# Dealing the index score matmuls of block 2 among the products of the forget-gate load

## What is computed

```
h = rmsnorm_2(x, norm_mix[layer])
hq, hf, hi, hg, sq, sk, sv, iq, ik, iw, mq = split_in(h @ w_in[layer])
...
# sparse attention: which 128 keys a query keeps
s = jnp.einsum('bqhd,bsd->bqhs', iqb, ik32)            # index scores, 8 heads of 64
score = jnp.einsum('bqh,bqhs->bqs', iwb, jax.nn.relu(s))
score = jnp.where(visible[None], score, -jnp.inf)
_, idx = lax.top_k(score, topk)
...
# recurrence: decay from the forget logit
z = f_logit.astype(f32)
log_f = jnp.logaddexp(jnp.log(lb), jnp.log1p(-lb) + jax.nn.log_sigmoid(z))
k = (1.0 - lb) * jax.nn.sigmoid(-z)
```

## Time and profile before

| | |
|---|---|
| median of 3 runs | 1704.19 us |
| lowest and highest | 1703.19 and 1706.45 us |
| span of the profiled execution | 1701.9 us |
| profiled execution, outside of its span | not shown |
| TensorE busy | 1630.8 us, 96% |
| VectorE busy | 925.6 us, 54% |
| ScalarE busy | 620.5 us, 36% |
| mean granted TensorE clock | 0.957 |

### The profile page before, as it was taken

The page is one execution under the profiler, slowest core; times in us unless marked ns, Lnnn a source line. Parts: engine busy times, 40 slices in busy tenths (PEclk is TensorE's granted clock), DMA queues, the critical chain, the costliest instruction groups (busy, mean ns, idle before and its releaser), DMA issues.

```text
span 1701.9 us, 20773 instructions
## 1 busy us (share of the span) xinstructions
PE 1630.8 (96%) x7854; PEld 1342.2 (79%) x7854; DVE 925.6 (54%) x1471; ACT 620.5 (36%) x856; POOL 26.1 (2%) x17
## 2 busy tenths in 40 slices
PE   5999999999998999999999899899899999999999
PEld 5788666888876788888888668899668788888887
DVE  6343365644544777777334768888844444444322
ACT  6241333432233444444233355454334232222211
POOL 0000000000000000000001000110000000000000
PEclk9999999999998999999999999999558999999999
DMA  6402221222222122223323212022001222222332
GB/s 232 142 26 100 71 72 50 96 79 96 99 99 99 48 100 99 99 99 113 109 99 113 75 53 97 25 75 75 1 1 50 92 106 99 94 89 92 113 107 74
DMA packets 24890, 147.11 MB, mean 86 GB/s; under 512 B 2515, under 2 KB 5075, under 8 KB 8316
## 3 DMA queue, kind: packets, MB, share of 16 engines
q1 hardware_dynamic: 24828, 146.27, 24.7%
HBM read 144.13 MB, written 2.13 MB: 86 GB/s over the span
## 4 chain that ended last, share of the span: by engine, by line
PE 89%; DVE 5%; ACT 3%; issue 2%; DMA 0%; DVEq 0%; SPq 0%; ACTq 0%
PE bank L1537 26%; PE bank L1539 25%; PE bank L1538 25%; PE bank L1631 4%; PE bank L1649 3%; PE bank L1638 2%; PE bank L1881 1%; ACT w_hi L544 1%; PE bank L1851 1%; DVE w_lo L947 1%; PE bank L1660 1%; PE bank L1590 0%; DMA vec<-vec 0%; DVE diag L1001 0%; DVE h_lo L1016 0%
## 5 line engine op out<-in xcount | busy, mean ns | idle before, releaser
L947 DVE TENSOR_TENSOR w_lo<-raw,w_hi 128x2048 fp32r<-128x2048 f32 x123 | 281.8, 2291 | 400.6 <-ACT w_hi L544 400.3
L1537 PE MATMUL bank<-h_hi,w_hi 128*128 128x512 f32 (+1 forms) x1200 | 476.0, 397 | 11.1 <-DVE h_lo L1016 9.9
L1539 PE MATMUL bank<-h_hi,w_lo 128*128 128x512 f32 (+1 forms) x1200 | 470.1, 392 | 0.0
L1538 PE MATMUL bank<-h_lo,w_hi 128*128 128x512 f32 (+1 forms) x1200 | 469.7, 391 | 0.0
L544 ACT ACTIVATE w_hi<-raw 128x2048 fp32r<-128x2048 f32 x129 | 246.3, 1910 | 353.7 <-PE bank L1539 352.0
L1537 PEld LDWEIGHTS bank<-h_hi,w_hi 128*128 128x128 f32 (+1 forms) x1200 | 226.2, 188 | 65.1 <-DVE h_lo L1016 9.8
L1539 PEld LDWEIGHTS bank<-h_hi,w_lo 128*128 128x128 f32 (+1 forms) x1200 | 226.0, 188 | 49.1
L1538 PEld LDWEIGHTS bank<-h_lo,w_hi 128*128 128x128 f32 (+1 forms) x1200 | 226.3, 189 | 47.3 <-issue 1.0
L1537 PE MATMUL bank<-a_hi,w_hi 128*128 128x512 f32 x352 | 136.9, 389 | 0.0
L1538 PE MATMUL bank<-a_lo,w_hi 128*128 128x512 f32 x352 | 136.9, 389 | 0.0
L1539 PE MATMUL bank<-a_hi,w_lo 128*128 128x512 f32 x352 | 136.9, 389 | 0.0
(11 more groups left out here) (247 smaller groups left out, 2048.2 us busy)
## 6 DMA issues: line engine op xcount, KB each, us to landing
raw<-weights SPq DMA_DIRECT2D x129, 1024.0 KB, 4.8
toep<-bias_scratch SPq DMA_DIRECT2D x8, 448.0 KB, 4.6
x<-xT SPq DMA_DIRECT2D x1, 2048.0 KB, 14.7
outT<-x SPq DMA_DIRECT2D x8, 256.0 KB, 4.3
memT<-memT SPq DMA_DIRECT2D x1, 1024.0 KB, 5.9
mem2T<-mem2T SPq DMA_DIRECT2D x1, 1024.0 KB, 5.5
masks_in<-masks SPq DMA_DIRECT2D x1, 512.0 KB, 3.3
vec<-vec SPq DMA_DIRECT2D x1, 140.0 KB, 5.7
```

The source lines that it names most:

```text
L947: nc.vector.tensor_tensor(w_lo[m % 2][:, :], raw[m % 2][:, :], w_hi[m % 2][:, :].bitcast(F32), ALU.subtract).then_inc(lo_ready, 1)
L1537: nc.tensor.matmul(o, lh, rh, start=first, stop=False)
L1538: nc.tensor.matmul(o, lh, rl, start=False, stop=False)
L1539: return nc.tensor.matmul(o, ll, rh, start=False, stop=last)
```

## The change

On TensorE each of the 24 index matmuls is followed by one product of `hf` (three fp32r matmuls), and the 8 products that are left come behind the last. On ScalarE the second `hf` load is rounded ahead of the third relu instead of behind the last. On VectorE that load is split in two halves, ahead of the fourth and of the sixth sum, instead of in one piece behind the causal adds.

```diff
--- before
+++ after
@@ ScalarE
             for w, (i, h) in enumerate(IDX):
+                if w == 2:
+                    round_w(FIRST["hf"] + 1)
                 ready(("idx", w))
                 if w >= 2:
                     act.wait_ge(relu_used, w - 1)
...
-            round_w(FIRST["hf"] + 1)
             for m in range(2):
                 round_w(FIRST["hf"] + m + 2)
@@ VectorE
             for w, (i, h) in enumerate(IDX):
                 keys = P * (i + 1)
+                if w in (3, 5):
+                    split_part(FIRST["hf"] + 1, w // 2 - 1)
                 wait_free(("idx", w))
...
             for m in range(2):
-                if m == 0:
-                    split_w(FIRST["hf"] + 1)
                 for t in (2 * m, 2 * m + 1):
                     ready(("hf", t))
@@ TensorE
             wait_all("ik", range(1))
+            def forget_product(p_):
+
+                t, kt = divmod(p_, KT)
+                ld, cs = FIRST["hf"] + t // 2, slice(t % 2 * P, (t % 2 + 1) * P)
+                if kt == 0:
+                    weights(ld)
+                    claim(("hf", t))
+                ins = product(B(("hf", t))[:, :], w(ld, 1)[:, kt, cs], w(ld, 0)[:, kt, cs], h_hi[:, kt, :],
+                              h_lo[:, kt, :], kt == 0, kt == KT - 1)
+                if kt == KT - 1:
+                    done(("hf", t), ins)
+
             for w_, (i, h) in enumerate(IDX):
                 claim(("idx", w_))
 
                 done(("idx", w_), nc.tensor.matmul(B(("idx", w_))[:, 0:P * (i + 1)], iq[:, h // 2, i * P:(i + 1) * P],
                                                    ik[h % 2][:, 0:P * (i + 1)], start=True, stop=True))
-            feature_loads("hf", 2)
+                forget_product(w_)
+            for p_ in range(len(IDX), 4 * KT):
+                forget_product(p_)
             feature_loads("hq", 2)
```

## The result

Kernel after: median 1708.70 us of 15 runs (1703.52 to 1710.41). Kernel before beside it: 1704.19 us of 15 runs (1703.19 to 1706.47). The ratio is 1.0022, with a 95% interval of 1.0015 to 1.0030: slower by 3.8 us at the ratio, 4.5 us between the medians. 1709.0 was forecast. The profiled execution took 1708.07 us with a span of 1706.3 us, 4.4 more than before.

A forecast was written before the change was run, and what follows sets the result against it. The prediction took TensorE to bound the kernel (busy 1630.8 of 1701.9 us). Level 0 starting 5.3 us later, less 0.5 for its clock, gave 4.8: span 1706.7, plus 2.3 around it, 1709.0 us; range 1705.0 to 1712.0.

The forecast's parts named there:

- standstill: Index stage: TensorE waits at product 0 for VectorE's split of the first forget load, 1.55 us.
- switches: Index stage: TensorE changing between fp32 and fp32r 24 times costs 0.03 us a step, 0.7 us in all.
- low stretch in the stage: Index stage: TensorE's clock stays low until 994.9 because of idle time inside the stretch, 1.25 us more lost.
- stall for the query load: Behind the forget products: TensorE waiting for the first query load's split, a tie, nothing or at worst 0.5 us.
- hand-over: Ahead of the first level: VectorE lets ScalarE go for its table load at 1064.5 instead of 1058.5, 6.0 us later.
- exponentials end, z begins +4.4: First level: ScalarE's exponentials end at 1068.1, behind the masked copies, so VectorE begins z 4.4 us later.
- pair of z halves: First level: VectorE's two halves of z start together with GpSimd's suffix sum and take 4.55 us, 0.95 more.
- level 0's clock: First level: after the longer TensorE standstill the low clock costs 2.5 us instead of 3.0, 0.5 less.
- Short low stretch: Rival, index stage: the clock comes back as soon as before, 1.7 us less, 1707.3 us; chance 25%.
- Costly switches: Rival, index stage: 0.09 us or more per fp32/fp32r change plus 0.5 query load stall, 1711.0 us; chance 15%.
- Lateness hidden: Rival, first level: VectorE's lateness leaves no trace, only TensorE's own 1.8 to 3.5 us stay, about 1706.5; chance 10%.
- The last attention's clock: Rival, from 1200 us: full clock returns inside the 85 us low stretch, 3.35 us back per 6.7, 1700.5; chance 5%.

The follow-up runs named there:

- rounds inside: Kernel after, with query tile 1's causal row added behind the eighth sum and ten of its selection rounds among sums 8 to 17: 1706.54 us.
- diagonal early in after: Kernel after, with TensorE's 32 diagonal products between the second and third query tile instead of behind all four: 1708.14 us.
- products from 2 on: Kernel after, with products dealt from the third index matmul on and ten left behind the last: 1705.79 us.
- early hand-over: Kernel after, with VectorE telling ScalarE to go on ahead of its last five selection rounds instead of behind them: 1704.93 us.
- early hand-over in before: Kernel before, with VectorE telling ScalarE to go on ahead of its last five selection rounds: 1703.16 us.
- TensorE as before: Kernel after, with all 24 index matmuls first again on TensorE; ScalarE's and VectorE's edits stay: 1704.95 us.
- products from 8 on: Kernel after, with the first product behind the ninth index matmul, 16 dealt and 16 left behind the last: 1704.77 us.
- three together: Kernel after, with products from 2 on, early hand-over and rounds inside combined: 1701.26 us.
- all together: Kernel of three together, plus diagonal products early and the last ten selection rounds ahead of the last two query tiles: 1696.64 us.
- diagonal early, before: Kernel before, with the early hand-over and TensorE's 32 diagonal products between the second and third query tile: 1697.86 us.

## Why the prediction was right, step by step

Each step with what was forecast, and what it measured (the 0.22 us at the start subtracted where it is a time):

| step | forecast | measured |
|---|---|---|
| product 0 starts | 989.0 | 988.95 |
| standstill | 1.55 us | 1.5 us (index matmul 0 through after 0.43) |
| switches | 0.03 us each, 0.7 | 0.02 each, 0.5 (1022.32 - 1020.77 = 1.55; 0.853 + 0.68 without) |
| low stretch in the stage | to 994.9, 1.25 more | 6.9 us long, to about 995; held, see below |
| last index matmul ends | 1023.4 | 1022.95 |
| last sum ends | 1025.0 | 1024.54 |
| stall for the query load | none, at worst 0.5 | none (its first product at 1029.32, 0.24 behind the last of `hf`) |
| hand-over | 1064.5, +6.0 | 1063.81, +5.2 |
| exponentials end, z begins +4.4 | 1068.1 | 1067.27, z +3.6 |
| pair of z halves | 4.55 us | 4.97 us |
| level 0 starts | 1072.8, +5.3 | 1072.38, +4.95 |
| level 0's clock | 0.5 less | 0.7 less |
| span | +4.8 | +4.4 |

**The mechanism held**, and experiments show its parts. VectorE's idle time was not removed but moved to where it is no use (rounds inside: 2.2 us back; diagonal early in after: nothing back). The standstill is in the chain (products from 2 on: 2.9 us back, 1.4 of the chain being the two products). The exponentials came last and met GpSimd (early hand-over: 3.8 us back). The three overlap on one chain, so their sum is more than the 4.5 us they explain. The 3.8 us may hold some of the attention's clock, which came back early in that profile (1.6 us) and in an unknown share of its other runs.

**Sizes that were off.** The list on VectorE took 1064.03 - 1024.76 = 39.3 us for 39.5. The hand-over was 0.7 us earlier than forecast, 0.46 of it since the last sum ended earlier (the switches and the standstill were cheaper), 0.23 from the list. The collision was mis-sized the other way, 4.97 for 4.55: I took a later level for it, where GpSimd took 3.36 us; here it took 3.77. That is the whole difference, since the second half of z ends 1.09 us behind GpSimd's sum there (1097.82 for 1096.73) and 1.08 behind it here. The sum itself gets shorter from level to level: where no half of z starts with it, it takes 2.82 us at level 0 in before and 2.06 at level 4 (1123.98). The Trainium skill ("GPSIMD Engine Reference", 1. Specifications) says only that the two contend; the price comes from such rows.

The sum landed within 0.4 us of the span partly by luck. z began 0.8 us less late than forecast and its two halves took 0.4 us longer, which cancels half of it; level 0's clock was taken from the middle of a range of 1.7 to 3.35 us and not worked out. The forecast's own bounds don't come out of its terms either: with the switches at 0 to 2.2 us and the clock's term as stated it would be 1708.3 to 1710.5, and with the short stretch down to 1706.6, not 1707.5.

**The clock term, argued in the prediction.** I took the low stretch to be long because TensorE stands still inside it. In the twelve executions it has two lengths. Six have the short form (clock 0.89 over 985 to 1000: before, early hand-over in before, TensorE as before, products from 8 on, three together, all together). Six have the long one (0.77 or 0.78: after and the other five). Two of the long ones have no standstill inside the stage, "products from 2 on" and "diagonal early, before", the second with no product dealt at all.

```profile
985.00:1000.00 15.00, 13.91 (x38) 9.34 (x39) 11.20 (x18) 9.09 (x21) 0.00 (x0) 0.77 0.20 70
```

What goes with the length in all twelve is what TensorE did when the clock fell. In the six short ones it was working through the index matmuls. In the six long ones it stood idle: in after at product 0, in the other five ahead of the first index matmul. In "products from 2 on", for one, the clock over 986 to 987 is 0.52, and the index matmuls begin at 986.78. The closest pair is after and "TensorE as before". Their index matmuls began at 987.23 and 987.19, and the clock fell at the same time in both, about 988.4. In after TensorE was idle for the whole microsecond:

```profile
988.00:989.00 1.00, 0.00 (x0) 0.00 (x0) 1.00 (x1) 0.32 (x1) 0.00 (x0) 0.70 0.07 16
```

In "TensorE as before" it was busy for all of it (clock 0.69). There the full clock was back at 991.8 (0.60 over 991 to 992), in after at 995.2. So in this execution the step held for the reason given, with one execution on each side to show it. It is not a rule for other places. At level 0 ten executions have a low stretch, and the clock fell in TensorE's wait in all of them, yet in three (both early hand-overs and three together) it was back after 3.4 us; there it fell within the last half microsecond of the wait.

Whether another execution of after would have the short form is not shown, since it has one profile. Among the twelve the clock fell between 0.8 us ahead of the first index matmul and 1.2 us behind it, and that matmul itself began between 985.7 and 989.2, with nothing changed upstream. What sets either was not found. The rule that I cited from the Trainium skill ("TensorE: Matmul & The Clock Gate", part 1), that executions of one kernel differ in this, would take several profiles of one kernel to test; the spread between kernels that are alike up to this point fits it.

**The rivals.** Short low stretch: not what this execution shows. Costly switches: refuted (0.02 us, and "products from 8 on" costs nothing). Lateness hidden: refuted, level 0 moved with the hand-over. The last attention's clock does return earlier in some kernels and gives 1.6 us, by a low stretch of 85 us for 92 to 95; I had reckoned pieces of 3.35 and only in after. The profiled execution of "diagonal early, after" took 1703.7 us where that kernel's median is 1708.1. Against the profile of after it began the index matmuls 1.5 us earlier, took 1.25 us less up to the transposes (0.9 of it up to level 0) and 1.6 us less behind them: together the 4.3 us by which its span is shorter. I take it that the spread of after's own runs (1703.5 to 1710.4) has the same source, but this is argued: after has one profile.

**What stays open**: what sets the moment at which the clock falls in the index stage; when the clock of the last attention returns early (it did in four profiles: early hand-over in after, three together, and both with the diagonal early; early hand-over in before and all together, which reach it sooner than some of these, show none of it); and whether preparing the second load early costs 0.9 us or nothing.

## What to carry to other kernels

An engine that keeps pace with TensorE through one stage and has a fixed list behind it must be counted with it: TensorE work inserted into the stage moves that engine's idle time to a place where it is no use, unless something of its list moves along. Look at the wait ahead of the next stage (4.40 us here) and at the engine whose instruction ends it: dealing 16 products behind the last 16 index matmuls cost and gave nothing, while an earlier hand-over and earlier diagonal products gave some 7 us. Where an instruction of one engine waits out an instruction of another, as z does with the suffix sum here, let the other go first, beside work that it doesn't hold up (the selection rounds beside it in "early hand-over" took 0.54 us and 0.56 us as without it).

## What the runs showed of the hardware

- VectorE and GpSimd: two halves of z take 2.35 us alone (1064.97 to 1067.32) and 4.97 us when GpSimd's suffix sum starts with them (1067.52 to 1072.49); GpSimd takes 3.77 us for 2.88. They take turns: in all twelve executions, at every level, a half of z that is under way when the suffix sum ends is itself through 1.08 or 1.09 us later (1072.49 for 1071.41 here).
- Switching TensorE from an fp32 matmul to three fp32r matmuls and back costs 0.02 us (a step of 1.55 us against 1.533 by its parts).
- 32 matmuls of 128 columns in fp32 take 3.74 us at the full clock and 5.24 to 6.68 us at the start of a level that follows a standstill of 3.1 to 6.2 us. The longer standstill does not give the longer time: 3.12 us gave 5.24 to 5.41, 4.40 gave 5.93 to 6.68, 5.12 gave 6.33, and 6.14 and 6.17 gave 5.98 and 5.48. After a wait of 0.44 us they took 3.84, at the full clock.
- A low stretch of 85 to 95 us exists with TensorE busy nearly all of it; its length differs by some 10 us between kernels whose work there is identical.
